# Seven block products in place of eight for the second gate and up weight chunk of a feed-forward layer

## The chip, the cores and the metric

One core of a Trainium2 chip runs the whole program in one launch. The metric is the device time of an execution in microseconds. TensorE (PE) does the matmuls, VectorE (DVE) and ScalarE (ACT) the elementwise work, GpSimd (POOL) very little here, and SyncE (SP) issues the transfers from HBM.

## The reference

Two blocks run one after the other on 512 tokens of 1024 features. The change lies in the second block, in its feed-forward layers, of which there are four (two layers of the model, two each). Cut to what matters:

```python
D_FF = 2816

def swiglu(x, w_gate, w_up, w_down):
    return (jax.nn.silu(x @ w_gate) * (x @ w_up)) @ w_down

for l in range(DEPTH):                       # DEPTH = 2
    f = swiglu(rmsnorm(x, ffn1_pre_g[l]), ffn1_w_gate[l], ffn1_w_up[l], ffn1_w_down[l])
    x = x + FFN_RESIDUAL_WEIGHT * rmsnorm(f, ffn1_post_g[l])
    ...                                      # token mixing
    f = swiglu(rmsnorm(x, ffn2_pre_g[l]), ffn2_w_gate[l], ffn2_w_up[l], ffn2_w_down[l])
    x = x + FFN_RESIDUAL_WEIGHT * rmsnorm(f, ffn2_post_g[l])
```

All of it is float32.

## The kernel before

**Numbers in two parts.** TensorE reads a rounded type. Each operand of a large product is therefore held as a rounded part (`_hi`, made by ScalarE with a copy) and a remainder (`_lo`, made by VectorE with a subtraction), and `mm3` makes a product of three matmuls: hi x hi, hi x lo, lo x hi.

**Chunks.** The 2816 columns of the gate weights and of the up weights are read in 11 chunks `c` of 256 columns (1 MB each), in the order gate 0, up 0, gate 1, up 1 and so on. SP loads them into two raw buffers in turn; a load waits until the chunk two places before it has been split.

**Chunk 0: the first groups.** `first_groups` runs chunk 0 in two token halves of 256, since the last 128 tokens come late out of the stage before. Each half has four groups (gate and up, two column halves of 128 each) of 8 x 3 matmuls of 256 columns. Products land in PSUM; ScalarE applies silu to the gate's, VectorE multiplies with the up's (`up`, L2632).

**Chunk 1: plain.** For c = 1, `project` makes four groups of 8 x 3 matmuls of 512 columns.

**Chunks 2 to 10: seven block products.** A weight chunk (contraction 1024 x 256 columns) is seen as 2 x 2 blocks of 512 x 128, the tokens as 2 x 2 blocks of 512 x 256. Eight block products would give the result; `FAST_ORDER` makes it of seven, in the order 1, 6, 5, 7, 2, 3, 4. Each is 4 x 3 matmuls of 256 columns. One such chunk of gate or up is called a tile or key here. The products read combinations of blocks:

- Of the tokens: T1 to T4 (`mix_tokens` on VectorE, L2646 to L2655), once per layer. ScalarE rounds them (L1946), VectorE makes their remainders (L2749).
- Of each tile's weights: S1 and S2 (`first_mixed`, L2681, L2683), S3 and S4 (`last_mixed`, L2688, L2690); beside them A11, A12 (together "A1", L1918 and L2666) and A22 are read as they are. ScalarE rounds (L1918, L1924), VectorE makes remainders (L2666, L2674).

Products 1 and 2 read A11 and A12, 3 reads S4, 4 reads A22, 5 reads S1, 6 reads S2, 7 reads S3. Products 1, 2 and 3 read plain token blocks, 4 to 7 read T parts. ScalarE copies products 1, 6, 5 and 7 out of PSUM (`keep`), VectorE sums the results (L2696 to L2735).

**Order.** Each engine's order is the order of its program, written out by hand. In `ffn`, VectorE runs `first_groups` with `mix_tokens` in the middle of its second half, then chunk 1's splits, the token remainders, and the preparation of the first tile; the preparation of tile q + 1 stands inside the loop at tile q. On PE, product 1 waits for `w_lo_made[key, "A1"]`, product 6 for `w_lo_made[key, "S2"]` and, for the first tile, for the last token remainder. SP loads up to gate chunk 2 and then the two rows of gains of the layer before it goes on with up chunk 2.

Of the kernel before, what the change touches and what calls it, by code (L numbers as in the profile page):

```python
# [14 lines left out]
P = 128  # L15
D = 1024
KT = D // P
L = 512
# [40 lines left out]
TAIL = 4  # L59


FAST_FROM = 2
FAST_ORDER = ((1, "A11", "a"), (6, "S2", "b"), (5, "S1", "c"), (7, "S3", "b"), (2, "A12", "a"), (3, "S4", "c"), (4, "A22", "b"))
FAST_PLACE = {"A11": 0, "A12": 1, "A22": 2, "S1": 3, "S2": 4, "S3": 5, "S4": 6}
STARTS = {0: 0, 1: 512, 3: 896, 2: 1024}
# [176 lines left out]
PLAN, CHUNK = weight_plan()  # L242
# [8 lines left out]
def build(nc, A, out):  # L251
# [7 lines left out]
    with ctx:  # L259
# [238 lines left out]
        h_hi, h_lo = (main_hi, ctx_hi), (main_lo, ctx_lo)  # L498
# [303 lines left out]
        def tensor_program(pe):  # L802
            holder = {}
            rot = Ring(range(8))
# [20 lines left out]
            def begin(key):  # L825
                pe.wait_ge(*w_lo_made[key])
                return weights(key)

            def end(key):

                psum_full.values["used", key] = psum_full.count

            def project(event, w, j, n, hi, lo, off, width, ring):
                b = claim(ring.take(), event)
                for k in range(KT):
                    m = mm3(psum[0:n, b * BANK:b * BANK + width], w[0][:, k, j:j + n], w[1][:, k, j:j + n],
                            tokens(hi, k, off, width), tokens(lo, k, off, width), k == 0, k == KT - 1)
                done(m, event)
# [171 lines left out]
            for step in AB_STEPS:  # L1010
                kind = step[0]
                if kind == "v":
                    _, ch, t = step
                    w = begin(("ab_in", ch)) if t == 0 else weights(("ab_in", ch))
# [9 lines left out]
                elif kind == "mod":  # L1024
                    m = step[1] - 8
                    s = m % 3 if m < 12 else 0
                    pe.wait_ge(*late_landed[s][m])
                    late_product(8 + m, late_w[s], ring)
                elif kind == "group":
                    _, ch, j, r = step  # L1030
# [123 lines left out]
            for ch in range(8):  # L1154
                w = begin(("cd_in", ch))
# [169 lines left out]
            def ffn(f, layer, before, more):  # L1325
                s = ("ffn", f, layer)
                first_groups(before, [(("gate", s, j), ("gate", f, layer, 0), j) for j in range(2)] +
                             [(("up", s, j), ("up", f, layer, 0), j) for j in range(2)], s)
                for c in range(1, FAST_FROM):
                    for kind in ("gate", "up"):  # L1330
                        w = begin((kind, f, layer, c))
                        for j in range(2):
                            project((kind, s, 2 * c + j, 0), w, j * P, P, h_hi, h_lo, 0, L, rot)
                        end((kind, f, layer, c))
                rot.at = 0
                for q, key in enumerate(fast_keys(f, layer)):
                    banks = {}
                    for product, name, to in FAST_ORDER:
                        opens = to not in banks
                        if opens:  # L1340
                            banks[to] = claim(rot.take(), ("fast", s, q, to))
                        if product == 1:
                            pe.wait_ge(*w_lo_made[key, "A1"])
                        elif product == 6:
                            pe.wait_ge(*w_lo_made[key, "S2"])
                            if q == 0:
                                pe.wait_ge(*fast_t["lo", s])
                        elif product == 7:
                            pe.wait_ge(*fast_kept[s, q, "6"])
                            pe.wait_ge(*w_lo_made[key, "S3"])  # L1350
                        elif product == 2:
                            pe.wait_ge(*fast_kept[s, q, "1"])
                        elif product == 3:
                            pe.wait_ge(*fast_kept[s, q, "5"])
                            pe.wait_ge(*w_lo_made[key])
                        elif product == 4:
                            pe.wait_ge(*fast_kept[s, q, "67"])
                        w = fast_weights(key, name)
                        for k in range(4):
                            m = mm3(bank(banks[to], quarter), w[0][:, k, :], w[1][:, k, :], *fast_tokens(product, k), opens and k == 0, False)  # L1360
                        done(m, ("fast", s, q, product))
                    end(key)

                def ready(i, k, h):
                    if i == 0 and h == 0:
                        pe.wait_ge(*ff_ready(s, k))
                down(s, FT, *ff, ready, (lambda i: rms_turn(s, i)) if more else None)
# [177 lines left out]
        def scalar_program(act):  # L1545
# [24 lines left out]
            def split_at(c):  # L1570
                if c < len(PLAN) and PLAN[c][5]:
                    split_hi(key_of[c])
# [310 lines left out]
            def first_groups(before, sinks, split_after):  # L1883
                for half_ in range(2):
                    for n, sink in enumerate(sinks):
                        sink(half_)
                        if half_ == 0 and n == 0:
                            turn_square(before, 3)
                        if half_ == 0 and n == 1:
                            turn_hi(before, 3)  # L1890
                        if half_ == 1 and n == 1:
                            split_at(split_after)

            def ffn(f, layer, before, more):
# [3 lines left out]
                def gate(k, half_, n):  # L1898
                    event, u = ("gate", s, k, half_), len(used)
                    used.append((k, half_))  # L1900
                    if u > 2:
                        act.wait_ge(*gated["up", s, *used[u - 3]])
                    elif before == "cd":
                        act.wait_ge(*residual[max((e for e in work_order if work_number[e] % 3 == u), key=work_number.get)])
                    copy(work[u % 3][:, 0:n], event, full(event, n), silu_made, func=ACT.Silu)
# [30 lines left out]
                    act.activation(ff_hi[:, 2 * c:2 * c + 2, :], ff_plain[:, 2 * c:2 * c + 2, :], ACT.Copy).then_inc(*ff_hi_made.mark(("ff", s, c)))  # L1936

                sinks = [lambda half_, j=j: gate(j, half_, LC) for j in range(2)] + [lambda half_: None] * 2
                first_groups(before, sinks, CHUNK["gate", f, layer, 1])
                for c in range(1, FAST_FROM):  # L1940
                    split_at(CHUNK["up", f, layer, c])
                    for j in range(2):
                        gate(2 * c + j, 0, L)
                act.wait_ge(*fast_t["mixed", s])
                for i in range(4):
                    act.activation(t_hi[:, i, :, :], t_plain[:, i, :, :], ACT.Copy).then_inc(*fast_rounded.mark((s, i)))  # L1946
# [164 lines left out]
        def vector_program(dve):  # L2111
# [8 lines left out]
            def split_at(c):  # L2120
                if c < len(PLAN) and PLAN[c][5]:
                    split_lo(key_of[c])
# [500 lines left out]
            def ffn(f, layer, before, more):  # L2623
# [13 lines left out]
                def mix_tokens():  # L2637

                    def block(k_half, half_):
                        return [t[:, 4 * k_half:4 * k_half + 4, half_ * quarter:(half_ + 1) * quarter].bitcast(F32) for t in (main_hi, main_lo)]  # L2640

                    t1, t2, t3, t4 = [t_plain[:, i, :, :] for i in range(4)]
                    b11, b21 = [wide[i][:, :].rearrange("p (k n) -> p k n", k=4) for i in range(2)]
                    dve.wait_ge(*h_lo_made["rt", before, NT - 1, 1])
                    for dst, b in ((t1, block(0, 1)), (b11, block(0, 0)), (t3, block(1, 1)), (b21, block(1, 0))):
                        m = dve.tensor_tensor(dst, b[0], b[1], ALU.add)  # L2646
                    m.then_inc(*fast_t.mark(("plain", s)))
                    dve.wait_ge(*fast_t["plain", s])
                    dve.tensor_tensor(t3, t3, t1, ALU.subtract).then_inc(*fast_t.mark(("T3", s)))
                    dve.wait_ge(*fast_t["T3", s])  # L2650
                    dve.tensor_tensor(t1, t1, b11, ALU.subtract)
                    split_at(CHUNK["gate", f, layer, 1])
                    dve.tensor_tensor(t2, t3, b11, ALU.add).then_inc(*fast_t.mark(("T2", s)))
                    dve.wait_ge(*fast_t["T2", s])
                    dve.tensor_tensor(t4, b21, t2, ALU.subtract).then_inc(*fast_t.mark(("mixed", s)))  # L2655
# [85 lines left out]
                    dve.tensor_tensor(ff_lo[:, at, :], ff_plain[:, at, :], ff_hi[:, at, :].bitcast(F32), ALU.subtract).then_inc(*ff_lo_made.mark(("ff", s, c)))  # L2741

                sinks = [lambda half_: None] * 2 + [lambda half_, j=j: up(j, half_, *HALVES[half_]) for j in range(2)]
                first_groups(before, sinks, CHUNK["gate", f, layer, 1], mix_tokens)
                for c in range(1, FAST_FROM):
                    split_at(CHUNK["up", f, layer, c])
                for i in range(4):
                    dve.wait_ge(*fast_rounded[s, i])
                    m = dve.tensor_tensor(t_lo[:, i, :, :], t_plain[:, i, :, :], t_hi[:, i, :, :].bitcast(F32), ALU.subtract)  # L2749
# [4 lines left out]
                last_mixed(keys[0])  # L2754
                for name in ("S1", "S2"):
                    lo_mixed(keys[0], name)
                up(2 * FAST_FROM - 2, 0, 0, L)
                for name in ("S3", "S4"):
                    lo_mixed(keys[0], name)
                up(2 * FAST_FROM - 1, 0, 0, L)  # L2760
                for q, key in enumerate(keys):
                    following = keys[q + 1] if q + 1 < len(keys) else None
                    if q:
# [362 lines left out]
```

## Time and profile before

| | us |
|---|---|
| median of 2 runs | 2556.09 (2556.0 to 2556.18) |
| profiled execution | 2556.28 |
| its span | 2554.5 |
| PE busy | 2528.2 |
| DVE busy | 1596.8 |
| ACT busy | 1164.2 |

The span is the time from the first to the last instruction in the profile; some 1.8 us of the execution lie around it. Matmuls are pipelined, so the time of one in the trace (0.28 us for 256 columns) is longer than the distance from one start to the next (0.12 us).

### The profile page before, as it was taken

How to read it: one execution, taken by the hardware profiler on the slowest of the kernel's cores; microseconds unless marked ns; L12 is line 12 of the kernel's file. 1: busy time of each engine (PE TensorE's matmuls, PEld its weight loads, DVE VectorE, ACT ScalarE, POOL GpSimd, SP SyncE). 2: the span in 40 equal slices, each digit the busy share in tenths (PEclk: the TensorE clock that was granted, in tenths of full speed). 3: DMA queues.
4: the chain of work that ended last, by engine and by line, in shares of the span. 5: the costliest groups of instructions: out<-in, count | busy, mean ns of one | idle time of the engine just before them, and what ended most of it. 6: DMA issues, size and time to landing. Idle time of an engine off the chain costs nothing.

```text
span 2554.5 us, 42046 instructions
## 1 busy us (share of the span) xinstructions
PE 2528.2 (99%) x17260; PEld 2203.4 (86%) x17260; DVE 1596.8 (63%) x2811; ACT 1164.2 (46%) x2015; POOL 167.7 (7%) x272
## 2 busy tenths in 40 slices
PE   9999999999999999999999999999999999999998
PEld 7788887678999888877999988999888877899987
DVE  3425653668898343367799735899444357699833
ACT  4223333642555334476455533555334467365522
POOL 0240010001000001012000000000000112100000
PEclk9999999999999999999999999999999999999999
DMA  8722141112333223211233332333233211333321
GB/s 327 293 95 76 57 116 42 34 59 68 98 107 109 99 84 103 71 63 67 83 116 100 116 103 79 116 100 116 99 99 104 67 51 42 116 100 100 116 99 66
DMA packets 183853, 252.72 MB, mean 99 GB/s; under 512 B 13040, under 2 KB 158448, under 8 KB 179184
## 3 DMA queue, kind: packets, MB, share of 16 engines
q1 hardware_dynamic: 183664, 250.04, 29.9%
q8 instruction: 138, 2.26, 0.4%
q14 instruction: 51, 0.42, 0.1%
HBM read 247.92 MB, written 2.10 MB: 98 GB/s over the span
## 4 chain that ended last, share of the span: by engine, by line
PE 93%; DVE 3%; ACT 1%; issue 1%; DMA 1%; POOL 0%; SPq 0%; POOLq 0%; DVEq 0%; ACTq 0%
PE psum L818 90%; PE psum L1387 1%; DMA mod_w<-in_l_ab_w_mod 1%; PE psum L1270 1%; PE psum L886 1%; DVE stats_first L2218 0%; DVE work L2211 0%; DVE X L2214 0%; ACT work L1616 0%; ACT w_hi L1568 0%; POOL stats_first L2948 0%; PE psum L862 0%; PE psum L1519 0%; DVE ff_lo L2741 0%; DVE w_lo L2117 0%
## 5 line engine op out<-in xcount | busy, mean ns | idle before, releaser
L818 PE MATMUL psum<-h_hi,w_hi 128*128 128x256 f32 (+1 forms) x1520 | 498.8, 328 | 0.3 <-DVE w_lo L2117 0.3
L818 PE MATMUL psum<-h_hi,w_lo 128*128 128x256 f32 (+1 forms) x1520 | 490.2, 322 | 0.0
L818 PE MATMUL psum<-h_lo,w_hi 128*128 128x256 f32 (+1 forms) x1520 | 490.1, 322 | 0.0
L2117 DVE TENSOR_TENSOR w_lo<-raw,w_hi 128x2048 fp32r<-128x2048 f32 (+1 forms) x99 | 223.6, 2263 | 309.7 <-ACT w_hi L1568 309.1
L818 PEld LDWEIGHTS psum<-h_hi,w_hi 128*128 128x128 f32 x1520 | 289.5, 190 | 30.2 <-issue 7.0
L818 PEld LDWEIGHTS psum<-h_hi,w_lo 128*128 128x128 f32 x1520 | 289.3, 190 | 22.6
L818 PEld LDWEIGHTS psum<-h_lo,w_hi 128*128 128x128 f32 x1520 | 289.6, 191 | 21.1 <-issue 1.4
L1568 ACT ACTIVATE w_hi<-raw 128x2048 fp32r<-128x2048 f32 (+1 forms) x100 | 188.2, 1887 | 246.3 <-PE psum L818 236.0
L818 PE MATMUL psum<-w_hi,ff_hi 128*128 128x512 f32 x576 | 224.9, 390 | 1.3 <-DVE ff_lo L2741 1.3
L818 PE MATMUL psum<-w_lo,ff_hi 128*128 128x512 f32 x576 | 224.1, 389 | 0.0
L818 PE MATMUL psum<-w_hi,ff_lo 128*128 128x512 f32 x576 | 224.1, 389 | 0.0
L818 PE MATMUL psum<-ff_hi,w_hi 128*128 128x256 f32 x1152 | 213.2, 283 | 0.0
L1918 ACT ACTIVATE w_hi<-raw 128x1024 fp32r<-128x1024 f32 (+1 forms) x144 | 120.9, 842 | 172.4 <-PE psum L818 172.4
L818 PEld LDWEIGHTS psum<-ff_hi,w_hi 128*128 128x128 f32 x1152 | 179.3, 191 | 0.0
L818 PE MATMUL psum<-w_hi,h_hi 128*128 128x256 f32 (+2 forms) x512 | 166.6, 325 | 0.6 <-DVE h_lo L2150 0.5
L818 PE MATMUL psum<-ff_hi 128*128 128x256 f32 (+1 forms) x992 | 165.3, 297 | 0.0
L818 PE MATMUL psum<-ff_hi,w_lo 128*128 128x256 f32 x576 | 162.9, 283 | 0.0
L1930 ACT ACTIVATE wide<-psum 128x256 f32<-128x256 f32 x288 | 110.4, 383 | 114.4 <-PE psum L818 101.0
L818 PE MATMUL psum<-w_lo,h_hi 128*128 128x256 f32 (+2 forms) x512 | 158.3, 309 | 0.0
L818 PE MATMUL psum<-w_hi,h_lo 128*128 128x256 f32 (+2 forms) x512 | 158.3, 309 | 0.0
L818 PEld LDWEIGHTS psum<-ff_hi 128*128 128x128 f32 x992 | 132.9, 191 | 5.0
L2666 DVE TENSOR_TENSOR w_lo<-raw,w_hi 128x1024 fp32r<-128x1024 f32 (+1 forms) x144 | 131.0, 951 | 0.0
(362 smaller groups left out, 5182.3 us busy)
## 6 DMA issues: line engine op xcount, KB each, us to landing
raw<-in_ffn_w_gate SPq DMA_DIRECT2D x44, 1024.0 KB, 5.3
raw<-in_ffn_w_up SPq DMA_DIRECT2D x44, 1024.0 KB, 5.4
raw<-in_ffn_w_down SPq DMA_DIRECT2D x44, 1024.0 KB, 4.8
raw<-in_w_in SPq DMA_DIRECT2D x36, 512.0 KB, 5.1
raw<-in_l_ab_w_in SPq DMA_DIRECT2D x10, 1024.0 KB, 9.3
mod_w<-in_l_ab_w_mod SPq DMA_DIRECT2D x8, 1024.0 KB, 17.7
raw<-in_w_out SPq DMA_DIRECT2D x8, 1024.0 KB, 4.9
raw<-in_cd_w_in SPq DMA_DIRECT2D x7, 1024.0 KB, 5.6
```

Of the source, the lines that this page charges most:

```text
L818: return pe.matmul(o, lhsT, rhs, start=start, stop=stop, skip_group_check=True)
L886: m = pe.transpose(bank(b, P, j * P), wide[1][:, k * P:(k + 1) * P], ident[:, :])
L1270: m = pe.transpose(bank(b + k // 4, P, (k % 4) * P), probs[(n - 1) % 2][:, k * P:(k + 1) * P], ident[:, :])
L1387: m = pe.transpose(bank(b, P, k * P), src[:, k * P:(k + 1) * P], ident[:, :])
L1568: act.activation(split_tiles(key)[0][:, 0:nk * n], raw[c % 2][:, 0:nk * n], ACT.Copy).then_inc(*w_hi_made.mark(key))
L1918: act.activation(dst, src, ACT.Copy).then_inc(*w_hi_made.mark((key, name)))
L1930: act.activation(fast_stage(q, name), bank(b, quarter), ACT.Copy).then_inc(*fast_kept.mark((s, q, name)))
L2117: dve.tensor_tensor(lo[:, 0:nk * n], raw[c % 2][:, 0:nk * n], hi[:, 0:nk * n].bitcast(F32), ALU.subtract).then_inc(*w_lo_made.mark(key))
L2666: dve.tensor_tensor(dst, src, hi.bitcast(F32), ALU.subtract).then_inc(*w_lo_made.mark((key, name)))
```

## The change

`FAST_FROM` goes from 2 to 1: chunk 1 joins the chunks that are made of seven block products, and a layer then has 20 tiles instead of 18. The plain loops for chunk 1 leave PE, ACT and DVE, and with them its plain splits, one of which stood inside `mix_tokens` and one of which stood in `first_groups` on ScalarE. Nothing is put in their place between the first groups and the preparation of the first tile.

```diff
-FAST_FROM = 2
+FAST_FROM = 1
...
 (PE, ffn)
-                for c in range(1, FAST_FROM):
-                    for kind in ("gate", "up"):
-                        w = begin((kind, f, layer, c))
-                        for j in range(2):
-                            project((kind, s, 2 * c + j, 0), w, j * P, P, h_hi, h_lo, 0, L, rot)
-                        end((kind, f, layer, c))
                 rot.at = 0
...
 (ACT, ffn)
-                first_groups(before, sinks, CHUNK["gate", f, layer, 1])
-                for c in range(1, FAST_FROM):
-                    split_at(CHUNK["up", f, layer, c])
-                    for j in range(2):
-                        gate(2 * c + j, 0, L)
+                first_groups(before, sinks, None)
                 act.wait_ge(*fast_t["mixed", s])
...
 (DVE, mix_tokens)
                     dve.tensor_tensor(t1, t1, b11, ALU.subtract)
-                    split_at(CHUNK["gate", f, layer, 1])
                     dve.tensor_tensor(t2, t3, b11, ALU.add).then_inc(*fast_t.mark(("T2", s)))
...
 (DVE, ffn)
-                first_groups(before, sinks, CHUNK["gate", f, layer, 1], mix_tokens)
-                for c in range(1, FAST_FROM):
-                    split_at(CHUNK["up", f, layer, c])
+                first_groups(before, sinks, None, mix_tokens)
...
                 for name in ("S1", "S2"):
                     lo_mixed(keys[0], name)
-                up(2 * FAST_FROM - 2, 0, 0, L)
                 for name in ("S3", "S4"):
                     lo_mixed(keys[0], name)
-                up(2 * FAST_FROM - 1, 0, 0, L)
```

## Rows read from the trace of the kernel before

**Rows 1.** The page: busy times by engine, and the granted clock in 40 slices.

```profile
PE 2528.2 (99%) x17260; PEld 2203.4 (86%) x17260; DVE 1596.8 (63%) x2811; ACT 1164.2 (46%) x2015; POOL 167.7 (7%) x272
...
PEclk9999999999999999999999999999999999999999
```

**Rows 2.** Chain of waits: start us, length us, what; two feed-forward layers.

```profile
617.66 215.96 PE psum L818 x1716
...
2209.13 215.95 PE psum L818 x1716
```

**Rows 3.** Windows, first layer: the plain chunk 1, then the first two tiles.

```profile
core 0: us, PE busy (x) PEld busy (x) DVE busy (x) ACT busy (x) POOL busy (x), PEclk, DMA share, GB/s
631.90:653.68 21.78, 21.78 (x98) 18.02 (x97) 13.33 (x16) 10.35 (x13) 0.00 (x0) 1.00 0.43 145
653.68:663.76 10.08, 10.08 (x86) 10.07 (x84) 10.04 (x17) 6.08 (x12) 0.00 (x0) 1.00 0.32 105
```

**Rows 4.** Timeline of PE: start us, length us; handovers in the first and second layer.

```profile
631.78 0.28 PE L818 MATMUL psum<-h_hi,w_lo 128*128 128x256 f32 x1
631.90 0.40 PE L818 MATMUL psum<-h_hi,w_hi 128*128 128x512 f32 x1
...
653.68 0.28 PE L818 MATMUL psum<-h_hi,w_hi 128*128 128x256 f32 x1
...
663.76 0.28 PE L818 MATMUL psum<-h_hi,w_hi 128*128 128x256 f32 x1
...
1274.49 0.28 PE L818 MATMUL psum<-h_hi,w_hi 128*128 128x256 f32 x1
```

**Rows 5.** Timeline of DVE in the first layer.

```profile
626.90 1.23 DVE L2651 TENSOR_TENSOR ff_room<-ff_room,wide 128x1024 f32<-128x1024 f32 x1
628.62 2.29 DVE L2117 TENSOR_TENSOR w_lo<-raw,w_hi 128x2048 fp32r<-128x2048 f32 x1 [0.49 <-ACT w_hi L1568]
630.83 1.22 DVE L2653 TENSOR_TENSOR ff_room<-ff_room,wide 128x1024 f32<-128x1024 f32 x1
632.08 1.23 DVE L2655 TENSOR_TENSOR ff_room<-wide,ff_room 128x1024 f32<-128x1024 f32 x1
...
644.64 4.63 DVE L2749 TENSOR_TENSOR ff_hi<-ff_room,ff_hi 128x1024 fp32r<-128x1024 f32 x4 [8.24 <-ACT ff_hi L1946]
649.19 0.69 DVE L2681 TENSOR_TENSOR w_plain<-raw 128x512 f32<-128x512 f32 x1
...
650.52 1.82 DVE L2666 TENSOR_TENSOR w_lo<-raw,w_hi 128x1024 fp32r<-128x1024 f32 x2
...
653.46 0.68 DVE L2674 TENSOR_TENSOR w_lo<-w_plain,w_hi 128x512 fp32r<-128x512 f32 x1
654.06 0.69 DVE L2674 TENSOR_TENSOR ff_hi<-ff_room,ff_hi 128x512 fp32r<-128x512 f32 x1
...
655.26 1.29 DVE L2674 TENSOR_TENSOR ff_hi<-ff_room,ff_hi 128x512 fp32r<-128x512 f32 x2
```

**Rows 6.** Timeline of ACT in the first layer: the four token parts.

```profile
643.56 3.90 ACT L1946 ACTIVATE ff_hi<-ff_room 128x1024 fp32r<-128x1024 f32 x4
```

**Rows 7.** Timeline of DVE: where the preparation of tiles 1 to 4 begins.

```profile
657.06 0.69 DVE L2681 TENSOR_TENSOR w_plain<-raw 128x512 f32<-128x512 f32 x1
...
665.41 0.68 DVE L2681 TENSOR_TENSOR w_plain<-raw 128x512 f32<-128x512 f32 x1
...
675.41 0.69 DVE L2681 TENSOR_TENSOR w_plain<-raw 128x512 f32<-128x512 f32 x1
...
684.43 0.68 DVE L2681 TENSOR_TENSOR w_plain<-raw 128x512 f32<-128x512 f32 x1
```

**Rows 8.** End of the span: the last matmul, then PE's windows (busy, clock, DMA).

```profile
2546.36 0.39 PE L818 MATMUL psum<-ff_hi,ff_lo 128*128 128x512 f32 x1
...
2550.00:2551.00 1.00, 0.00 (x0) 0.99 0.00 0
2551.00:2552.00 1.00, 0.00 (x0) 0.50 0.00 0
```

**Rows 9.** Timeline of SP's DMA queue in the first layer, and landings there.

```profile
630.94 0.37 SPq L662 DMA_DIRECT2D raw<-in_ffn_w_gate  x1
631.35 0.58 SPq L760 DMA_DIRECT2D post_g<-in_ffn_post_g  x1
...
636.43 0.38 SPq L662 DMA_DIRECT2D raw<-in_ffn_w_up  x1
656.58 0.38 SPq L662 DMA_DIRECT2D raw<-in_ffn_w_gate  x1
...
raw<-in_ffn_w_gate SPq DMA_DIRECT2D x1, 1024.0 KB, 5.4
```

More of the change, by code:

```diff
@@ L1890, in first_groups @@
                             turn_hi(before, 3)
-                        if half_ == 1 and n == 1:
+                        if half_ == 1 and n == 1 and split_after:
                             split_at(split_after)
```

## Prediction

> **What bounds the kernel now.** First the page's busy times: TensorE is at work for 2528.2 us of the 2554.5 us span, VectorE for 1596.8, and the granted clock of TensorE is at its upper level (2.4 GHz, a 9 in the page) in every slice [rows 1]. Then the chain of waits, which shows where TensorE's time can be shortened: in each feed-forward stage it holds one piece of TensorE alone, about 216 us and 1716 matmuls long, of which the first begins at 617.66 and the last at 2209.13 [rows 2]. So in these four stages nothing but matmuls sets the end, and the cover behind which VectorE and ScalarE prepare is complete. A change there pays one for one in TensorE time saved, and costs one for one in any time that TensorE must then stand.
>
> **Part 1, the matmuls.** The reader compares three stretches of the windows view. Chunk 1 by plain products takes 21.78 us for gate and up together, and each of the two following weight tiles by seven block products takes 10.08 us [rows 3]. By the code the plain chunk has 2 kinds x 2 column halves x 8 contraction tiles x 3 passes = 96 matmuls of 512 columns, 21.78 / 96 = 0.227 us each; one tile by blocks has 7 x 4 x 3 = 84 matmuls of 256 columns, 10.08 / 84 = 0.120 us each. The starts of the matmuls agree: 631.90, 653.68 and 663.76 us [rows 4]. The change puts 2 x 84 matmuls of 256 columns where 96 of 512 were: 20.16 us for 21.78, a gain of 1.62 us per feed-forward stage, 4 x 1.62 = 6.5 us in all. That is 12.5% fewer columns, but only 7.4% less time, as 256 columns cost more than half of 512.
>
> The Trainium skill (TensorE: Matmul & The Clock Gate, Back-to-back issue gap) puts an isolated gap at N / 2.4 + 2.5 ns, so 216 ns and 109 ns; by it a stage would gain 96 x 0.216 - 168 x 0.109 = 2.4 us and all four 9.6 us. The trace has 227 and 120 ns, and the trace is used.
>
> **Part 2, the cover that goes.** Chunk 1's plain matmuls, 21.78 us, stand between the end of the first groups (chunk 0) and the first block product. Under them ScalarE and VectorE make what the block products read: the rounded and remainder parts of the four token combinations, and of the first tile's seven weight blocks. Afterwards chunk 0's second token half alone is ahead of them, and that is too late to begin much. I replay VectorE's queue for the first stage, with the times of the trace.
>
> Token sums. The four sums and T3 have run by 626.9 and t1 runs from 626.90. Then stands the remainder of gate chunk 1 (628.62, 2.29 us, with 0.49 us of wait before it), then T2 at 630.83 and T4 at 632.08, done at 633.31 [rows 5]. Without that remainder T2 begins at 628.1 and T4 is done near 630.5. ScalarE rounds the four token parts in 3.90 us [rows 6], now from 630.5 to 634.5, the first of them ready at 631.6. It needs no weight split ahead of that any more, as both of chunk 1's splits are gone.
>
> The queue's next item is the gating of chunk 0's second half. Its last product is issued at 631.78 and ends at 632.06 (0.28 us), so VectorE is done with it at about 632.5. This instruction is late for a reason that the change doesn't touch: it waits for TensorE's last plain matmul. Behind it are queued, in this order, the four token remainders (644.64 to 649.19 in the trace, 4.55 us), the first two sums of weights, the remainder of A11 and A12, that of A22, the last two sums, and the remainders of S1 and S2 [rows 5]. Measured from 649.19: A11 and A12 are ready after 2.25 us (the pair at 650.52 takes 1.82, the first of them 0.93), S2 after 5.55 us (the pair S1 at 653.46 and S2 at 654.06, 0.69 each). From 632.5 + 4.55 = 637.05 this gives product 1 at 639.3 and product 6, which reads S2, at 642.6.
>
> TensorE is free at 631.90. So it stands 7.4 us ahead of product 1. That product takes 12 x 0.120 = 1.44 us, and then TensorE stands 642.6 - 640.75 = 1.85 us more. S3, S4 and the kept products come 0.6 us apart behind S2 (655.26, two in 1.29 us, and the 0.6 us gating between them is gone [rows 5]), while a product takes 1.44, so nothing stands after that. Key 0 ends at 642.6 + 72 x 0.120 = 651.25.
>
> The second tile: its preparation begins on VectorE at 657.06 in the trace [rows 7], 3.4 us after product 1 and 1.9 after product 6 could start; now it begins at about 643.8, 1.2 us after product 6, so it is no later than it was. From there the work is the trace's own, with a period of 8.4 to 10.0 us of VectorE (665.41, 675.41, 684.43 [rows 7]) under TensorE's 10.08. Key 1 ends at 661.3, where the trace has the same work (chunk 1 done) at 653.68. **Cost of a stage at full clock: 7.6 us**, which is 9.25 us of standing less the 1.62 us of part 1.
>
> The other three stages have the same handovers (1274.49 for the second [rows 4]); the queues are the same code, and I take the same price. 4 x 7.6 = 30.4 us.
>
> **Part 3, the clock.** Nowhere in the trace does TensorE stand as long in mid-kernel. Only at the end is there such a row: the last matmul starts at 2546.36 and ends at 2546.75, the granted clock is still 0.99 in 2550 to 2551 and is 0.50 (1.2 GHz) in 2551 to 2552, so it fell 4.2 us after the last matmul [rows 8]. A stand of 7.4 us is longer, so I expect it to fall in each stage, near 636, and product 1 to start at 1.2 GHz. It then takes up to 2.9 us and ends at 642.2, still ahead of S2 at 642.6: that loss is free. What follows costs until the clock is back. No row shows how long that takes. Ends: 0, when it is back before 642.6; 8.64 us, when all of the other 72 matmuls run at half clock. I take the row that is nearest, the 4.2 us of the fall, from 639.3 to 643.5: 0.9 us at half clock lose 0.45 us. 4 x 0.45 = 1.8 us.
>
> That idle time lowers the clock and the next burst starts slow is also what the Trainium skill says (same page, HAM oscillation: how this bites in real kernels); it speaks against this change.
>
> **Part 4, transfers.** SP's queue loads gate chunk 2 (630.94) when gate chunk 1 is split, then the two gain rows (631.35), then up chunk 2 (636.43) [rows 9]. Gate chunk 2 now waits for S4 of the first tile, about 643.8, and needs some 5.4 us: the first such load in the trace to start after a tile of blocks is at 656.58 for a sum at 665.41, 8.8 us later [rows 7, 9]. It lands near 650 to 651, with the gains beside it, and VectorE asks for it near 652. One to two us of cover on VectorE and more on TensorE: cost 0, and up to 2 us a stage if the gains slow it.
>
> **Sum.** The profiled execution took 2556.28 us (span 2554.5 and 1.8 around it), 0.2 us over the median of the runs. 2556.3 + 30.4 + 1.8 = 2588.5 us, 1.3% slower.
>
> **Rivals.**
> A, the cover suffices (faster): the point that decides is whether S2's remainder is ready when TensorE is free, at 631.90. If VectorE's queue of 4.55 + 5.55 us were done before, all of 6.5 us would be gained: 2549.8 us. Only the token part could run ahead, and its remainders stand in program order behind the last gating, at 632.06. Against it: [rows 5]. Chance 3%.
> B, the clock stays low (slower still): it comes back only after products 6, 5 and 7, 4.3 us of work that take 8.6: 4.3 us a stage beyond 30.4, 2603.9 us; if the whole first tile is slow, 8.6 a stage, 2621 us. For it: no row shows a return of the clock. Against it: the work after S2 is unbroken. 13%, of which 5% beyond 2607.
> C, the late load of gate chunk 2 adds a second stand of up to 2 us a stage: 2596.5 us. 7%.
> D, smaller stands than replayed: VectorE starts the token remainders earlier, or the changed list leaves other than 20 block tiles; half the standing would give 2556.3 - 6.5 + 4 x 4.6 = 2568.2 us. The list is built from `FAST_FROM`, so the tiles are certain; the order is fixed. 5%.
> Forecast: 72%.
>
> **Range and chances.** Around the forecast, the replay can be off by 1 us a stage (4 us) and the clock by 0 to 2.9 us a stage (two products at half clock). 2580 to 2605 us takes in C and the first price of B (8%), and leaves out A, D and the long end of B, 13%. What a measurement of this kernel can tell from no change is about 2%, 51 us: faster 1%, within 93%, slower 6% (the far end of B).
>
> **What would show it.** The windows of the changed kernel: two tiles of blocks where one plain pair was, 20 tiles a stage; TensorE idle for 7 to 8 us ahead of the first block product and for 0.4 to 2 us ahead of the second, with VectorE's remainder of A11 and A12 as releaser; granted clock of 0.5 around those idle stretches and 1.0 elsewhere; ScalarE's rounding of tokens done before VectorE's token remainders; no DMA ended wait on TensorE. I am wrong if TensorE's idle time in a stage is under 5 or over 12 us.

## The result, and the profile after

The changed kernel takes 2588.5 us (two runs, 2587.7 and 2589.3) where the kernel before takes 2556.09: a ratio of 1.0128, 95% interval 1.0103 to 1.0152, slower by 32.4 us. In a later series it was 2590.14 against 2556.21 (four executions, 2589.57 to 2590.53; ratio 1.0131, interval 1.0116 to 1.0147). Its profiled execution took 2589.3 us with a span of 2587.5, 33.0 more than the span before.

The page of the changed kernel, busy times and clock, against [rows 1]:

```profile
PE 2529.9 (98%) x17548; PEld 2218.6 (86%) x17548; DVE 1649.0 (64%) x2923; ACT 1190.2 (46%) x2087; POOL 167.1 (6%) x272
```

TensorE has 288 matmuls more and is busy for about the same time, so the change's own saving is not visible in this row, and the longer span is not its work. The list of what TensorE waited for has a new first row (engine line waited for: us in total, times, longest us):

```profile
PE psum L818 <- DVE w_lo L2655: 30.7, 4, 7.7
PE psum L818 <- DMA ident<-in_k_ident: 3.4, 1, 3.4
```

Four waits of 7.7 us for VectorE's remainder of A11 and A12 (L2655 here, L2666 before). The chain of waits, whose one piece for each layer had 1716 matmuls [rows 2], now breaks at each of them and goes on with product 6 of the first tile:

```profile
642.29 199.93 PE psum L818 x1656
...
1272.06 199.15 PE psum L818 x1656
...
1630.05 199.32 PE psum L818 x1656
...
2259.39 198.75 PE psum L818 x1656
```

TensorE's timeline in the first layer, against [rows 4]: the last plain matmul, product 1, product 6, and the starts of the second and third tile.

```profile
631.37 0.28 PE L818 MATMUL psum<-h_hi,w_lo 128*128 128x256 f32 x1
...
639.33 0.55 PE L818 MATMUL psum<-h_hi,w_hi 128*128 128x256 f32 x1 [7.67 <-DVE w_lo L2655]
...
642.29 2.87 PE L818 MATMUL psum<-ff_hi 128*128 128x256 f32 x12
...
652.20 0.29 PE L818 MATMUL psum<-h_hi,w_hi 128*128 128x256 f32 x1
...
662.27 0.28 PE L818 MATMUL psum<-h_hi,w_hi 128*128 128x256 f32 x1
```

A plain matmul of 256 columns gives way to the next after 0.12 us, so TensorE was free at 631.49. It reached product 6 after 10.80 us, finished the first tile 9.91 us later and the second after another 10.07: 30.78 us, where chunk 1 took 21.78 [rows 3].

VectorE's timeline, against [rows 5]: the last gating, the four token remainders, the first sum of weights, A11, A12 and A22, the last of S1 and then S2 to S4, and the start of the second tile's preparation.

```profile
631.76 0.42 DVE L2622 TENSOR_TENSOR ff_plain<-work,psum 128x256 f32<-128x256 f32 x1 [1.31 <-PE psum L818]
632.10 4.62 DVE L2736 TENSOR_TENSOR ff_hi<-ff_room,ff_hi 128x1024 fp32r<-128x1024 f32 x4
636.64 0.68 DVE L2670 TENSOR_TENSOR w_plain<-raw 128x512 f32<-128x512 f32 x1
...
637.96 1.82 DVE L2655 TENSOR_TENSOR w_lo<-raw,w_hi 128x1024 fp32r<-128x1024 f32 x2
...
641.51 1.89 DVE L2663 TENSOR_TENSOR ff_hi<-ff_room,ff_hi 128x512 fp32r<-128x512 f32 x3
643.31 0.68 DVE L2670 TENSOR_TENSOR w_plain<-raw 128x512 f32<-128x512 f32 x1
```

From the gating on it has no gap: what waits is TensorE, on a queue without slack. Between 623 and 650 us its only idle time is the 1.31 us ahead of the gating, where it waits for TensorE's last plain product. The windows of TensorE in the same stretch (busy, granted clock, DMA share, GB/s) show the clock:

```profile
632.00:640.00 8.00, 0.68 (x3) 0.67 0.00 0
640.00:646.00 6.00, 5.94 (x32) 0.58 0.23 66
646.00:652.00 6.00, 6.00 (x52) 1.00 0.81 287
```

Here and below, the stand is the time in which TensorE waits ahead of products 1 and 6. The clock fell to its lower level (0.50, which is 1.2 GHz) within it, near 634.7, and was back near 645.0, 5.7 us after product 1 had started. In the other three layers it was back 3.9, 4.4 and 3.1 us after product 1's start. Product 6's 12 matmuls began under it: 644.99 - 642.29 = 2.70 us against 1.44.

### The profile page after: what moved, and what is told of

The parts are those of the page before. It is cut to its first block, busy times and chain, and to the rows that moved or that the text cites. A ratio compares the mean times of both kernels' runs of the same rounds, so it can differ in the third digit from the quotient of the medians.

```text
span 2587.5 us, 42854 instructions
## 1 busy us (share of the span) xinstructions
PE 2529.9 (98%) x17548; PEld 2218.6 (86%) x17548; DVE 1649.0 (64%) x2923; ACT 1190.2 (46%) x2087; POOL 167.1 (6%) x272
## 4 chain that ended last, share of the span: by engine, by line
PE 92%; DVE 4%; issue 1%; ACT 1%; DMA 1%; POOL 0%; SPq 0%; POOLq 0%; DVEq 0%; ACTq 0%
PE psum L818 89%; PE psum L1381 1%; DMA mod_w<-in_l_ab_w_mod 1%; PE psum L1270 1%; PE psum L886 1%; DVE ff_hi L2736 1%; DVE stats_first L2208 0%; DVE work L2201 0%; DVE X L2204 0%; ACT work L1610 0%; ACT w_hi L1562 0%; POOL stats_first L2933 0%; PE psum L862 0%; PE psum L1513 0%; DVE ff_lo L2730 0%
## 5 line engine op out<-in xcount | busy, mean ns | idle before, releaser
L818 PE MATMUL psum<-h_hi,w_hi 128*128 128x256 f32 (+1 forms) x1456 | 469.8, 323 | 31.0 <-DVE w_lo L2655 30.7
L818 PE MATMUL psum<-h_hi,w_lo 128*128 128x256 f32 (+1 forms) x1456 | 460.6, 316 | 0.0
L818 PE MATMUL psum<-h_lo,w_hi 128*128 128x256 f32 (+1 forms) x1456 | 460.4, 316 | 0.0
L2107 DVE TENSOR_TENSOR w_lo<-raw,w_hi 128x2048 fp32r<-128x2048 f32 (+1 forms) x91 | 205.3, 2260 | 306.7 <-ACT w_hi L1562 306.7
L1562 ACT ACTIVATE w_hi<-raw 128x2048 fp32r<-128x2048 f32 (+1 forms) x92 | 172.9, 1885 | 231.1 <-PE psum L818 221.4
L818 PE MATMUL psum<-ff_hi,w_hi 128*128 128x256 f32 x1280 | 236.9, 283 | 0.0
L818 PEld LDWEIGHTS psum<-ff_hi,w_hi 128*128 128x128 f32 x1280 | 199.3, 191 | 0.0
L818 PE MATMUL psum<-ff_hi,w_lo 128*128 128x256 f32 x640 | 181.0, 283 | 0.0
L818 PE MATMUL psum<-ff_hi 128*128 128x256 f32 (+1 forms) x1088 | 180.6, 299 | 0.2
L2655 DVE TENSOR_TENSOR w_lo<-raw,w_hi 128x1024 fp32r<-128x1024 f32 (+1 forms) x160 | 145.5, 951 | 0.0
```

What stands on the lines that cost most here:

```text
L818: return pe.matmul(o, lhsT, rhs, start=start, stop=stop, skip_group_check=True)
L1562: act.activation(split_tiles(key)[0][:, 0:nk * n], raw[c % 2][:, 0:nk * n], ACT.Copy).then_inc(*w_hi_made.mark(key))
L2107: dve.tensor_tensor(lo[:, 0:nk * n], raw[c % 2][:, 0:nk * n], hi[:, 0:nk * n].bitcast(F32), ALU.subtract).then_inc(*w_lo_made.mark(key))
L2655: dve.tensor_tensor(dst, src, hi.bitcast(F32), ALU.subtract).then_inc(*w_lo_made.mark((key, name)))
```

## The experiments

They ran in three series (four, four and two kernels), each on one chip beside the kernel before (medians of 2556.2 to 2556.3 us in all series). Times of runs of different series are compared by way of that. The changed kernel itself came out at 2588.5 and at 2590.1 us, so differences of 1 to 2 us between series tell nothing.

**The clock (e1_awake, e7_changed_again, e8_awake_28).** Is the low clock a main part of the loss?

```diff
                 rot.at = 0
+                pe.wait_ge(*freed.get(holder[4], (psum_full.sem, 1)))
+                for _ in range(32):
+                    mm(bank(4, P), ones[:, :], ones[:, :], True, True)
                 for q, key in enumerate(fast_keys(f, layer)):
```

> The changed kernel, with 32 small matmuls of ones into a free PSUM bank between the first groups and the first block product of each feed-forward layer, so that TensorE works through the stand. My theory: the stand is VectorE's and stays (first block product about 7.8 us behind the last plain matmul, product 6 at 10.8); only the clock's share goes, which the traces put at 1.3, 0.5, 0.7 and 0.1 us in the four layers, 2.5 us in all: 2586 us. Rival, the low clock is a main part of the loss: some 4 us a layer come back, 2572 us. If the small matmuls themselves delay product 1, it starts later than 7.9 us behind the last plain matmul.

Measured: 2588.59 us. The expectation of 2586 was missed in the time and met in the layers. Its chain:

```profile
642.65 198.70 PE psum L818 x1656
...
1272.76 198.70 PE psum L818 x1656
...
1630.33 198.71 PE psum L818 x1656
...
2258.93 198.70 PE psum L818 x1656
```

At the full clock the piece that begins with product 6 is 198.70 us. Against that the changed kernel's four have 1.23 + 0.45 + 0.62 + 0.05 = 2.35 us more, which is the clock's share of its loss. The stand stays: TensorE is free at 631.84 and product 6 starts at 642.65, 10.81 us later for 10.80 before. So product 1, which ran at the full clock here, had lost nothing at the low one. The time did not follow. In the profiled execution the clock was low for a moment elsewhere, in the token mixing ahead of the second layer; the other three executions were not profiled, and why their times (2587.6 to 2588.9 us) are no lower is not shown:

```profile
1160.00:1164.00 4.00, 2.80 (x21) 1.00 0.01 2
1164.00:1168.00 4.00, 4.00 (x18) 0.57 0.02 4
```

From the first layer's `down` to product 6 of the second layer it took 429.69 us (1272.76 - 843.07) where the changed kernel took 428.12 (1272.06 - 843.94), 1.57 us more. It was therefore run again, with 28 small matmuls, beside the changed kernel.

> The changed kernel itself, unchanged, beside the next one on the same chip: 2588.5 us, with the clock low at each of the four stands.

> As e1_awake with 28 small matmuls instead of 32. In e1_awake the pieces of the chain behind product 6 all fell to 198.70 us (2.35 us less in all), but one short low stretch of the clock in the token mixing took 1.6 us in its profile. Theory: the clock's share of the change is 2.4 us, and that other stretch has nothing to do with it and comes or stays away by itself: 0.5 to 2.5 us below the changed kernel of this job. Rival: the low clock costs nothing that the median shows, the two are equal within 0.3 us.

Measured: 2590.14 us for the changed kernel and 2587.59 us with 28 small matmuls, 2.55 us apart, and no low stretch until the end in the latter's profile. The changed kernel's chain in this series:

```profile
643.28 198.72 PE psum L818 x1656
...
1271.90 199.89 PE psum L818 x1656
...
1630.65 199.74 PE psum L818 x1656
...
2260.32 199.03 PE psum L818 x1656
```

Over 198.70 these are 0.02 + 1.19 + 1.04 + 0.33 = 2.58 us. The share of a single layer changes from execution to execution, from 0.02 to 1.23 us, while both sums are near 2.5. So the clock costs some 2.5 us, under a tenth of the loss.

**The first product's weights ahead of the tokens (e2_a1_first).** What decides, the wait of product 1 or that of product 6?

```diff
 (DVE)
+                for name in ("A1", "A22"):
+                    lo_blocks(keys[0], name)
                 for i in range(4):
                     dve.wait_ge(*fast_rounded[s, i])
                     ...
                 first_mixed(keys[0])
-                for name in ("A1", "A22"):
-                    lo_blocks(keys[0], name)
```

> The changed kernel with the remainders of A11, A12 and A22 of the first tile made ahead of the token remainders, and their rounded parts ahead of the tokens' on ScalarE. Nothing is done less. Theory: what decides is when S2's remainder is ready, behind all of VectorE's queue; product 1 starts near 633.1 instead of 639.3, but product 6 still near 642.3, and the time stays within 1.5 us of 2588.5. Rival, each wait of TensorE is paid for by itself: 6.2 us a layer come back, 2564 us.

Measured: 2595.41 us, 6.8 us slower than the changed kernel of the first series and 5.3 slower than that of the later one (each against the kernel before). The rival is refuted, and the expected time, within 1.5 us of 2588.5, was missed as well. TensorE's timeline:

```profile
634.03 0.36 PE L818 MATMUL psum<-h_hi,w_hi 128*128 128x256 f32 x1 [1.81 <-DVE w_lo L2655]
...
642.87 2.90 PE L818 MATMUL psum<-ff_hi 128*128 128x256 f32 x12 [7.17 <-DVE ff_hi L2663]
```

Counted from when TensorE is free (632.07 here), product 1 starts after 1.96 us instead of 7.84, and product 6 after 10.80 us, as late as ever. Measured from the piece before it in the chain, product 6 is in the same place to 0.1 us (642.87 - 385.05 = 257.82; 642.29 - 384.51 = 257.78). The stand has only moved from ahead of product 1 to behind it, and there it costs more:

```profile
642.87 200.48 PE psum L818 x1656
...
1273.26 200.95 PE psum L818 x1656
...
1633.06 200.35 PE psum L818 x1656
...
2263.47 200.80 PE psum L818 x1656
```

These are 7.8 us over 4 x 198.70, where the changed kernel had 2.35. There product 1 ran under the low clock while TensorE had to wait for S2 anyway; here the clock stays low until 4.1 us after product 6's start (646.96 in the first layer), in work that is on the path.

**Preparation in the order of need (e3_by_need).** The same work of VectorE, each product waiting only for its own operands. ScalarE's rounding is put in a like order.

```diff
-(DVE) T1..T4 rem., sums S1 S2, A1, A22, sums S3 S4, S1, S2, S3, S4
+(DVE) A1, sums S1 S2, T2 rem., sums S3 S4, S2, T1 rem., S1, T3 rem., S3, A22, S4, T4 rem.
```

> The changed kernel with VectorE's preparation of the first tile in the order in which the products need it: A11 and A12, the sums for S1 and S2, the remainder of T2, the sums for S3 and S4, then the remainders of S2, T1, S1, T3, S3, A22, S4, T4; TensorE waits for each by itself. The same work. Replayed: product 6 starts near 636.0, the first tile ends near 645.3 instead of 652.2, 6.9 us earlier. If that were all, 2588.5 - 4 x 6.9 = 2561 us. My theory says that VectorE's total work bounds the second tile as well: S2 of the second tile is ready near 649.5 whatever the order, the second tile ends near 658.1 instead of 662.3, and about 3.5 to 4 us a layer come back: 2574 us.

Measured: 2577.53 us, 11.0 less than the changed kernel's first figure, 2.7 us a layer; 21.3 us above the kernel before. The span is 12.1 us shorter. The expected 2574 was missed by 3.5 us, the 2561 of a gain in the first tile alone by far. The chain shows which wait is the last one:

```profile
649.14 0.70 DVE h_lo L2670
649.83 0.14 issue
649.97 15.08 PE psum L818 x124
```

The first tile's product 6 started at 637.97, and the wait is now at product 6 of the second tile, for its S2, at 649.97; the replay had 649.5, which is some 2 us of the miss if the other three layers are like the first. The rest is not taken apart. VectorE's second tile begins at 643.60, as in the changed kernel (643.31). This order moves the stand; the sum of VectorE's work stays.

**Product 2 behind product 1 (e4_two_first).**

```diff
-                    for product, name, to in FAST_ORDER:
+                    for product, name, to in (FAST_ORDER if q > 1 else [FAST_ORDER[i] for i in (0, 4, 1, 2, 3, 5, 6)]):
```

> The kernel by need (the order of preparation from the experiment before), and in the first two tiles product 2 right behind product 1, since both read A11 and A12 alone: more of TensorE's work lies ahead of S2. Theory: VectorE's queue bounds the second tile, its S2 is ready at the same time as by need (18.5 us behind the last plain matmul); behind it only 5 products are left instead of 6, 1.44 us less a layer: 2577.5 - 5.8 = 2572 us. Rival, the first tile's order is what counts: it could end 1.4 us earlier too, and both together would give 2.9 us a layer, 2566 us.

ScalarE's copy of product 1 is moved forward with it. Measured: 2577.21 us, the same as e3_by_need within 0.3. Both expectations were missed. TensorE's timeline names another engine:

```profile
646.52 0.50 PE L818 MATMUL psum<-ff_hi,w_hi 128*128 128x256 f32 x2 [1.40 <-ACT wide L1928]
...
650.12 0.38 PE L818 MATMUL psum<-h_hi,w_hi 128*128 128x256 f32 x1 [0.47 <-ACT wide L1928]
```

Product 4 of the first tile waits for ScalarE's copy of product 7, and product 2 of the second tile for the copy of product 1. ScalarE's timeline says why the first is late: it stood 2.48 us for VectorE's sums of the second tile, ahead of the copy in its own order.

```profile
644.84 0.63 ACT L1922 ACTIVATE w_hi<-w_plain 128x512 fp32r<-128x512 f32 x1 [2.48 <-DVE w_plain L2681]
...
646.10 0.36 ACT L1928 ACTIVATE wide<-psum 128x256 f32<-128x256 f32 x1
```

So VectorE's lateness also reaches TensorE through ScalarE's queue, and the 1.4 us won in front were lost there.

**GpSimd takes two token remainders (e5_pool).**

```diff
+ (POOL)                for i in (2, 3):
+                            pool.wait_ge(*fast_rounded[s, i])
+                            pool.tensor_tensor(t_lo[:, i, :, :], t_plain[:, i, :, :], t_hi[:, i, :, :].bitcast(F32), ALU.subtract)
```

> As e4_two_first, and the remainders of T3 and T4 made by GpSimd instead of VectorE (two of 128 x 1024), with A11 and A12's remainder inside the token sums. It takes 2 x 1.14 = 2.3 us out of VectorE's queue, the same as nothing else was changed in it. Theory, VectorE's queue is the bound: S2 of the second tile comes 2.3 us earlier, 4 x 2.3 = 9 us: 2563 us, still above the kernel before, as VectorE has some 15 us of preparation ahead of S2 of the second tile where the first tile and products 1 and 2 of the second cover 13. Rival: GpSimd is slower (its 128 x 791 sum took 1.85 us, so some 2.3 us for 1024) and slows VectorE beside it, so that product 7 or 4 of the first tile waits for it and nothing is won: 2572 us.

Measured: 2589.43 us, 12.2 slower than e4_two_first. Neither expected time came near; the slowing of VectorE that the rival named did occur, and cost far more than it allowed for. The timelines of GpSimd and VectorE in the first layer:

```profile
634.43 5.33 POOL L3049 TENSOR_TENSOR ff_hi<-ff_room,ff_hi 128x1024 fp32r<-128x1024 f32 x2 [19.70 <-ACT ff_hi L1945]
```

```profile
634.67 2.88 DVE L2692 TENSOR_TENSOR ff_room<-raw 128x512 f32<-128x512 f32 x1
637.48 2.83 DVE L2694 TENSOR_TENSOR ff_room<-raw,ff_room 128x512 f32<-128x512 f32 x1
...
647.63 0.69 DVE L2692 TENSOR_TENSOR h_plain<-raw 128x512 f32<-128x512 f32 x1
```

The same instruction of VectorE (L2692, a sum of weights, 128 x 512) takes 0.69 us alone and 2.88 us beside GpSimd's. Two of them lost 2.88 + 2.83 - 2 x 0.69 = 4.3 us, more than the 2.3 us of work taken off. That is 2 us a layer; the rest of the 12.2 is not taken apart. Some of it is the clock, whose mean over the span is 0.993 here and 0.998 in e4_two_first. Each of the two lasted about as long as one of GpSimd's (5.33 / 2 = 2.67 us), so whether VectorE ran slower or waited for GpSimd's to end can't be told from these rows, and the factor of 4.2 belongs to this pair of sizes.

The Trainium skill (GPSIMD Engine Reference, Specifications) states that GpSimd shares its SBUF interfaces with VectorE and contends with its instructions of two SBUF inputs; the rows agree (2.88 us for 0.69).

**The gain alone (e6_one_more_plain).** The kernel before, with chunk 2 plain as well. With it VectorE's gatings and chunk 2's gate split are put in new places, which the lines below leave out.

```diff
-FAST_FROM = 2
+FAST_FROM = 3
```

> The kernel before, with chunk 2 plain as well (8 block products in place of 7), everything else in the same places: the gain of the seven products alone, with the sign turned and the cover kept. Theory: 96 matmuls of 512 columns in place of 168 of 256 cost 21.78 - 20.16 = 1.62 us a layer and no stand appears: 2556.1 + 6.5 = 2562.6 us. Rival, block tiles save 12.5 percent of the time as they save 12.5 percent of the columns (2.7 us a layer): 2567 us. Rival, they save nothing once the work around them is counted: 2556 us.

Measured: 2564.43 us, 8.2 us or 2.05 a layer above the kernel before. In the trace chunks 1 and 2 take from 632.10 to 675.64, 21.77 us each, so the price of plain against blocks is the 1.62 us expected. Another 0.33 is a stop ahead of product 6, since 0.45 us lie between the two starts below and a matmul takes 0.12. One gating (0.68 us) now stands ahead of S2's remainder. In the kernel before it stands behind, and product 6 follows product 1 there without a stop:

```profile
676.96 0.28 PE L818 MATMUL psum<-h_hi,w_lo 128*128 128x256 f32 x1
677.41 1.67 PE L818 MATMUL psum<-ff_hi 128*128 128x256 f32 x12 [0.17 <-issue]
```

**The token remainders left out (e9_no_token_remainders).** VectorE's four subtractions go as well, and product 6 waits for the rounding of the last token part instead.

```diff
-            return [t[:, {5: 0, 6: 1, 7: 2, 4: 3}[product], k, :] for t in (t_hi, t_lo)]
+            return [t[:, {5: 0, 6: 1, 7: 2, 4: 3}[product], k, :] for t in (t_hi, t_hi)]
```

> The changed kernel with the four token remainders left out (products 4 to 7 read the rounded token part in their place, so the output lacks these terms): 4.55 us less in VectorE's queue, TensorE's work the same. Theory, VectorE's queue sets the starts of product 1 and product 6 of the first tile: both come 4.55 us earlier in each layer, 3.3 and 6.3 us behind the last plain matmul; the second tile's S2 comes earlier by as much and it does not wait. With the shorter stand the clock may stay up. 2589 - 4 x 4.6 = 2571 us, down to 2568. Rival, something else (ScalarE's rounding, done 2.5 us behind the last plain matmul, or the load of the weights) is just behind: less than 2.5 us a layer, 2580 us or more.

Measured: 2578.16 us, 12.0 less than the changed kernel in its later series and 10.3 less than in the first, so 2.6 to 3.0 us a layer instead of 4.6. This is between the two expectations, near the rival's. The timelines of TensorE, VectorE and ScalarE:

```profile
636.86 0.55 PE L818 MATMUL psum<-h_hi,w_hi 128*128 128x256 f32 x1 [4.75 <-DVE w_lo L2655]
...
639.83 2.59 PE L818 MATMUL psum<-ff_hi 128*128 128x256 f32 x12
```

```profile
635.49 1.82 DVE L2655 TENSOR_TENSOR w_lo<-raw,w_hi 128x1024 fp32r<-128x1024 f32 x2 [1.52 <-ACT w_hi L1912]
```

```profile
630.61 3.90 ACT L1936 ACTIVATE ff_hi<-ff_room 128x1024 fp32r<-128x1024 f32 x4 [3.77 <-DVE ff_room L2644]
634.42 1.56 ACT L1912 ACTIVATE w_hi<-raw 128x1024 fp32r<-128x1024 f32 x2
```

VectorE now waits 1.52 us for ScalarE's rounding of A11 and A12, which stands in its order behind that of the tokens: 4.55 - 1.52 = 3.0 us a layer. From when TensorE is free (631.96), product 1 comes after 4.90 us and product 6 after 7.87 (3.3 and 6.3 were expected), each 2.9 us earlier than in the changed kernel. VectorE is the bound of the changed kernel, and ScalarE is 3 us behind it.

**No token combinations (e10_no_combinations).**

```diff
-                first_groups(before, sinks, None, mix_tokens)
+                first_groups(before, sinks, None, prepare_first)
```

Here `prepare_first` holds the weight work of the first tile, and `fast_tokens` gives plain token blocks to products 4 to 7.

> The changed kernel with no token combinations at all (products 4 to 7 read plain token blocks; the output is not that of the layer) and the first tile's weights prepared in their place, ahead of the last gating. TensorE's work is the same 168 matmuls of 256 columns. It shows what the change would be worth if the cover were enough. Theory: no stand, full clock, 2556.2 - 6.5 = 2549.7 us; by the measured price of one more plain chunk (8.2 us, of which 1.3 was a stop) down to 2548. Rival, the first tiles wait for something else too: above 2556 us.

Measured: 2549.98 us against 2556.29, ratio 0.9974 (0.9964 to 0.9985), 6.3 us faster; expected 6.5. The chain has its one long piece back, now with 1788 matmuls in 214.31 us where 1716 took 215.96 [rows 2]:

```profile
617.17 214.31 PE psum L818 x1788
```

No kernel that makes chunk 1 of block products and computes the whole layer beat the kernel before: the nearest, e4_two_first, is 21.0 us above it. VectorE's 1.31 us ahead of the last gating were used in e5_pool and e10_no_combinations alone; no run fills them in the whole layer without GpSimd.

## Why the prediction was right

The point forecast was 2588.5 us and the first measurement 2588.5. That they agree to the tenth is luck: the two executions behind it were 1.6 us apart, and the later series gave 2590.1. The mechanism came out as forecast. By its parts:

- **The bound.** Right: the four layers were pure TensorE, and e10_no_combinations shows the saving arriving one for one, while the changed kernel shows the stand being paid one for one.
- **Part 1, the saving.** 1.62 us a layer. e6_one_more_plain shows 21.77 us for a plain chunk, and the whole of it arrives as 6.3 of 6.5 us when nothing stands in its way. It is gained in the changed kernel too, only buried under the stand. The estimate of 9.6 us that the prediction drew from the Trainium skill (TensorE: Matmul & The Clock Gate, Back-to-back issue gap), with gaps of 109 and 216 ns, is not borne out: the rows have 120 and 227 ns, and e10_no_combinations gained 6.3 us.
- **Part 2, the cover.** The replay had 10.7 us from when TensorE is free to product 6 (631.90 to 642.6), measured 10.80; 7.4 us to product 1, measured 7.84, of which the trace calls 7.67 idle; second tile on time, and it was (643.31 for about 643.8, no wait behind product 6). Net at full clock: 10.80 + 8.64 + 10.08 - 21.78 = 7.74 us a layer for the 7.6 forecast. The second stand was there in the replay with 1.85 us; at the low clock product 1 filled all but 0.3 of it, near the 0.4 that the prediction had.
- **Part 3, the clock.** Right in kind, and in part lucky in size. The prediction had no row for the return and took the 4.2 us of the fall at the end of the span, the same in each layer; measured were 5.7, 3.9, 4.4 and 3.1 us, 4.3 in the mean. The loss was 1.23, 0.45, 0.62 and 0.05 us, 2.35 in all, for 4 x 0.45 = 1.8 forecast. Most of the difference is that product 6 started 2.96 us behind product 1 (642.29 - 639.33) where the replay had 3.3. That product 1 at the low clock was free is shown by e1_awake, where it ran at the full clock and product 6 started no earlier.
- **Part 4, the transfers.** Right: gate chunk 2 was issued at 643.42 and nothing on TensorE waited for a load.
- **The sum.** 4 x 7.74 + 2.35 = 33.3 us, and the spans differ by 33.0.
- **The rivals.** A failed for the reason given: the token remainders ran behind the last gating. B did not occur as priced: in the first layer the clock was low through the whole of product 6 and no further, 1.23 us for 4.3. C and D did not occur.

What the prediction did not see is what stands next in line. It spoke of VectorE's queue up to S2; e3_by_need and e4_two_first show that the same queue holds up the second tile as well, and ScalarE's order right behind it. The price in the changed kernel comes out of one replay, but the two reorderings tried get back only a third of it.

## What to carry to other kernels

Where a cheaper algorithm needs operands prepared by other engines, the dearer form ahead of it may be the cover for that preparation: compare the saving (here 1.62 us a layer) with the length of the preparation minus what cover is left (10.80 - 1.44 = 9.4 us, the way to product 6 less product 1's own work). A replay of the preparing engine's queue, instruction by instruction from the old trace, gave that to 0.2 us a layer. Then look at the second item, not the first alone: reordering moves a stand to wherever the queue's total work is due.

## What the runs showed of the hardware

- Subtractions with two inputs on GpSimd beside VectorE's sums: 0.69 us became 2.88 us, and GpSimd's own two subtractions of 128 x 1024 took 5.33 us. Work moved to the idle engine cost more than it took off.
- The stand costs more behind the burst of product 1 (e2_a1_first) than ahead of it: 7.8 us of low clock against 2.35 and 2.58 in the four layers.
- 28 small matmuls into a free PSUM bank in each stand kept the granted clock at its upper level and gave 2.55 us back (e8_awake_28); with 32 (e1_awake) the clock stayed up there as well, but no gain showed in the time.
- The clock can be low for a moment in a stage that a change does not touch (e1_awake and e5_pool, both 0.57 in 1164 to 1168; 1.6 us in the former), which is as large as differences one may want to read from a single execution.
